# Two transformer blocks on one core: the grouped attentions' value product, row totals, score minima and weight remainders changed

## The chip, the cores and the metric

The kernel runs on one core of a Trainium2 chip. The metric is the device time of one execution in microseconds; lower is better. Below, PE is TensorE, DVE VectorE, ACT ScalarE, POOL GpSimd, and SP the engine that only issues transfers.

## The reference

Two blocks work on x of 512 tokens by 1024 channels, all in float32. The first has one layer: an RMS norm, a projection to queries, keys, values and gates, attention "a" (8 query heads on 2 key heads of 64, a window of 128 to either side, a slope times the distance subtracted from the scores, and one sink logit per head that takes part in the softmax), attention "b" (8 heads, a neighbourhood of 8 rows by 16 columns, with a table of relative biases, no sink), gated merging, an output projection, and an MLP with a squared relu of width 4096. The second has two layers. Each is a gated MLP of width 2816, a mixer, and another gated MLP. The mixer has a causal attention "c0" or "c1" (8 heads on 2, window 128, slopes and sinks as in a) beside a gated short convolution. A norm ends it.

```python
sc = q @ k * scale - slope * dist          # -inf outside the window
p  = exp(sc - m) / (sum(exp(sc - m)) + exp(sink - m))
out = p @ v                                # p has 128 queries x up to 384 keys per block and head
```

## The kernel before, in words

Everything lies transposed: x is 8 tiles of 128 channels by 512 tokens. Each weight tile (a "unit", 128 rows by 1024 columns, 512 KB) is fetched by SP into one of three places `w_raw`, and split in two: ACT writes the rounded part `w_hi` (line 890), and the rest `w_lo` is the difference (line 1084 on DVE, job `split_v`; line 1341 on POOL, job `split_g`, which is used while attentions run). Activations are split in the same way, and a dense product is three fp32r matmuls per 128 rows: hi·hi, lo·hi, hi·lo (lines 765 to 767), eight such steps per result.

The order of all work is written out once by the class `Plan`. A "slot" is the gap after one dense step of three matmuls; `later(n, job)` puts a small job n slots ahead, between dense steps. Each engine then runs its share of the same list of jobs in order, and waits on semaphores where a job needs another engine's result. `next_unit` adds the fetch of the unit three ahead at once and its split one slot later, so that a tile is split at the start of the next unit and used two units after its place came free. SP's list has the fetches (line 1417) in the same order as its other transfers.

One attention goes block by block (4 blocks of 128 queries), in two groups of four heads, a group every 10 slots (`attend`). For a group: four `score` jobs (PE, lines 779 on; two banks), each followed on DVE by the bias and the slope, read from PSUM into `probs` (line 1261, for b line 1256); `softmax` on DVE (reduction to the row maximum L1269, maximum with the sinks L1273, negation L1275, sink shift L1278); `exps` on ACT (L1018, with the row sums); then per chunk of 128 keys `turn` (PE transposes four 128x128 pieces of the probabilities, L793; ACT copies them out, L1031) and `multiply` (L806), three slots later, with the turned probabilities standing and 64 columns of values streaming, head by head, in plain fp32. `normalise` (DVE, L1286 to L1294) multiplies the bank of both groups by the inverse totals, `turn_out` transposes the result back (PE L817, ACT L1036) and `y_lo` takes its remainder. Attention a has 10 chunks per group of heads, b 8, c0 and c1 7 each.

All four attentions run among projections: a from about 50 to 165 us, b from about 170 to 265, c0 from about 1130 to 1215, c1 from about 2030 to 2115. The first block's bias table for b is loaded over POOL's queue (L1369) at 32 to 41 us.

## Time and profile before

| | us |
|---|---|
| median of 3 runs (2530.28 to 2532.93) | 2532.54 |
| the profiled execution's own time | 2533.4 |
| its span, first to last instruction | 2531.6 |
| PE, DVE, ACT, POOL busy | 2499.9, 1251.5, 895.7, 261.3 |
| mean TensorE clock granted | 0.996 |

A row of a group gives the line, engine and operation, the tiles out<-in with partitions x elements, the count after x, the busy time and the mean of one, and then the time the engine sat idle before them with what released it. A row of a timeline gives start, duration and the same names. Records of matmuls overlap, because they are pipelined, so their durations are longer than their distance. The window view gives busy times per stretch, the granted clock as a share of 2.4 GHz, and the DMA engines' share.

### The profile page before, as it was taken

To read this page: it belongs to the slowest core of one execution; us is meant where nothing else is said; L and a number is where in the kernel's file an instruction comes from. 1 tells how busy PE (TensorE), PEld (TensorE's weight loads), DVE (VectorE), ACT (ScalarE), POOL (GpSimd) and SP (SyncE) were. 2 spreads that over 40 slices of the span, in tenths; PEclk is the share of its full clock that TensorE was granted. 3 is DMA by queue.
4 is the path that set the end of the run, shared out by engine and by line. 5 is a ranking of instruction groups with operands and counts; after the bars stand their busy time and mean duration, and the time that the engine had idled before them with its cause. 6 is when DMAs were issued, how large, how long until landed. Compare 5 with 4: busy or idle time off the path is not lost.

```text
span 2531.6 us, 28151 instructions
## 1 busy us (share of the span) xinstructions
PE 2499.9 (99%) x11504; PEld 2073.0 (82%) x11504; DVE 1251.5 (49%) x1555; ACT 895.7 (35%) x1347; POOL 261.3 (10%) x179
## 2 busy tenths in 40 slices
PE   8999999999999999999999999999999999999998
PEld 7878888888888888878888888888888788888886
DVE  6664455434475343466454444543444665544444
ACT  5556343223343222344432222422222444322222
POOL 3243110000030000013300000100000143000001
PEclk9999999999999999999999999999999999999999
DMA  6112333233223333232233232333232322332322
GB/s 166 50 56 62 107 110 100 92 100 100 88 87 108 96 96 100 83 102 67 83 100 99 93 100 86 99 100 100 92 100 86 99 75 76 100 100 92 100 90 77
DMA packets 71167, 235.36 MB, mean 93 GB/s; under 512 B 8832, under 2 KB 12544, under 8 KB 71040
## 3 DMA queue, kind: packets, MB, share of 16 engines
q1 hardware_dynamic: 69376, 230.36, 29.4%
q0 software_dynamic: 1664, 3.22, 0.7%
q8 instruction: 91, 1.49, 0.2%
q14 instruction: 36, 0.29, 0.0%
HBM read 231.35 MB, written 2.19 MB: 92 GB/s over the span
## 4 chain that ended last, share of the span: by engine, by line
PE 88%; DVE 5%; ACT 3%; issue 3%; POOL 1%; DMA 0%; SPq 0%; DVEq 0%; ACTq 0%; POOLq 0%
PE bank L765 28%; PE bank L767 28%; PE bank L766 28%; PE bank L806 2%; DVE w_lo L1084 2%; ACT w_hi L890 1%; PE bank L779 1%; PE bank L793 1%; DVE x L1200 1%; DVE z L1076 1%; ACT z L878 0%; POOL square_sum L1351 0%; DVE q L1151 0%; DVE kb_lo L1164 0%; ACT h_hi L900 0%
## 5 line engine op out<-in xcount | busy, mean ns | idle before, releaser
L765 PE MATMUL bank<-h_hi,w_hi 128*128 128x512 f32 x2224 | 880.3, 396 | 3.8 <-DVE h_lo L1099 1.5
L767 PE MATMUL bank<-h_hi,w_lo 128*128 128x512 f32 x2224 | 868.0, 390 | 0.0
L766 PE MATMUL bank<-h_lo,w_hi 128*128 128x512 f32 x2224 | 867.4, 390 | 0.0
L1084 DVE TENSOR_TENSOR w_lo<-w_raw,w_hi 128x1024 fp32r<-128x1024 f32 (+2 forms) x392 | 485.4, 1239 | 319.4 <-ACT w_hi L890 318.8
L890 ACT ACTIVATE w_hi<-w_raw 128x1024 fp32r<-128x1024 f32 (+1 forms) x435 | 448.8, 1033 | 400.3 <-PE bank L767 397.9
L765 PEld LDWEIGHTS bank<-h_hi,w_hi 128*128 128x128 f32 x2224 | 418.9, 188 | 88.6 <-DVE w_lo L1084 4.5
L767 PEld LDWEIGHTS bank<-h_hi,w_lo 128*128 128x128 f32 x2224 | 418.1, 188 | 88.5
L766 PEld LDWEIGHTS bank<-h_lo,w_hi 128*128 128x128 f32 x2224 | 419.0, 188 | 81.2 <-issue 1.7
L767 PE MATMUL bank<-act_hi,w_lo 128*128 128x512 f32 x960 | 373.5, 389 | 0.0
L766 PE MATMUL bank<-act_lo,w_hi 128*128 128x512 f32 x960 | 373.5, 389 | 0.0
L765 PE MATMUL bank<-act_hi,w_hi 128*128 128x512 f32 x960 | 373.5, 389 | 0.0
L1076 DVE TENSOR_TENSOR z<-bank,rms_inv 128x512 f32<-128x512 f32 x238 | 168.6, 710 | 296.6 <-PE bank L767 295.8
L1351 POOL TENSOR_TENSOR square_sum<-square_sum,z 128x512 f32<-128x512 f32 x55 | 73.8, 1342 | 1839.4 <-ACT z L878 1839.4
L1200 DVE SCALAR_TENSOR_TENSOR x<-bank,x 128x512 f32<-128x512 f32 x152 | 104.7, 689 | 282.8 <-PE bank L767 282.8
L766 PEld LDWEIGHTS bank<-act_lo,w_hi 128*128 128x128 f32 x960 | 180.2, 188 | 37.5
L765 PEld LDWEIGHTS bank<-act_hi,w_hi 128*128 128x128 f32 x960 | 180.2, 188 | 37.5
L767 PEld LDWEIGHTS bank<-act_hi,w_lo 128*128 128x128 f32 x960 | 180.2, 188 | 37.2
L1007 ACT ACTIVATE act_hi<-z 128x512 fp32r<-128x512 f32 x88 | 55.6, 632 | 389.6 <-DVE z L1221 389.6
L1002 ACT ACTIVATE z<-z 128x512 f32<-128x512 f32 x88 | 55.6, 632 | 285.3 <-DVE z L1076 285.3
L1341 POOL TENSOR_TENSOR w_lo<-w_raw,w_hi 128x1024 fp32r<-128x1024 f32 x51 | 123.3, 2421 | 265.4 <-ACT w_hi L890 265.4
L1084 DVE TENSOR_TENSOR act_lo<-z,act_hi 128x512 fp32r<-128x512 f32 x120 | 83.2, 693 | 105.0 <-ACT act_hi L1007 61.4
L900 ACT ACTIVATE h_hi<-x,gains 128x512 fp32r<-128x512 f32 x56 | 40.6, 724 | 126.7 <-DVE x L1200 122.2
(169 smaller groups left out, 1678.0 us busy)
## 6 DMA issues: line engine op xcount, KB each, us to landing
w_raw<-ffn_wg_dram SPq DMA_DIRECT2D x88, 512.0 KB, 3.5
w_raw<-ffn_wu_dram SPq DMA_DIRECT2D x88, 512.0 KB, 3.5
w_raw<-w_in_dram SPq DMA_DIRECT2D x67, 512.0 KB, 3.6
w_raw<-ffn_wd_dram SPq DMA_DIRECT2D x64, 512.0 KB, 3.5
w_raw<-w_up_dram SPq DMA_DIRECT2D x32, 512.0 KB, 3.6
w_raw<-w_down_dram SPq DMA_DIRECT2D x32, 512.0 KB, 3.8
w_raw<-w_out_dram SPq DMA_DIRECT2D x24, 512.0 KB, 3.6
w_raw<-ffn_wd_dram SPq DMA_DIRECT2D x32, 384.0 KB, 3.2
```

What stands on the lines that cost most here:

```text
L765: engine.matmul(to, w_hi[s][:, lhs], hi, start=k == 0, stop=False)
L766: engine.matmul(to, w_hi[s][:, lhs], lo, start=False, stop=False)
L767: product = engine.matmul(to, w_lo[s][:, lhs], hi, start=False, stop=job == "k_last")
L806: product = engine.matmul(value_bank[:, half(place(name, h))], turned[0:rows, n * P:(n + 1) * P], values[name][0:rows, chunk, value_head(n ...
L890: engine.activation(w_hi[s][:, 0:width], w_raw[s][:, 0:width], ACT.Copy).then_inc(signals["w_hi"].s, 1)
L1002: engine.activation(z[zs[1] % Z_RING][:, :], z[zs[0] % Z_RING][:, :], ACT.Silu).then_inc(signals["silued"].s, 1)
L1007: engine.activation(act_hi[:, plan.hidden[key] % FF_RING, :], z[zs[1] % Z_RING][:, :], ACT.Copy).then_inc(signals["act_hi"].s, 1)
L1076: engine.tensor_tensor(to, src, scale, ALU.mult).then_inc(signals["evacuated"].s, 1)
L1084: engine.tensor_tensor(lo, value, hi.bitcast(F32), ALU.subtract).then_inc(signals[event].s, 1)
L1200: engine.scalar_tensor_tensor(x[:, m, :], dense_bank[plan.results[r].bank][:, :], factor(r), x[:, m, :], ALU.mult, ALU.add).then_inc(signa ...
L1341: engine.tensor_tensor(w_lo[s][:, 0:width], w_raw[s][:, 0:width], w_hi[s][:, 0:width].bitcast(F32), ALU.subtract).then_inc(signals["w_lo_g ...
L1351: engine.tensor_tensor(to, to, z[zs % Z_RING][:, :], ALU.add).then_inc(signals["scaled_sum" if scaled else "square_sum"].s, 1)
```

## The change

It has five parts. They concern a, c0 and c1 ("grouped") unless b is named.

1. Value product. The values of one key head now stand in the array as a 128x128 tile, 64 columns of the rounded part beside 64 of the remainder, and the turned probabilities of four heads stream over it, 512 columns, first their rounded part, then their remainder (new job `turn_lo` on DVE after ACT's copy; `v_lo` for the values). The bank holds the product transposed already: the lower 64 rows hold the remainder of the values. Job `pair` (ACT copies the lower half out, DVE adds it to the upper) ends each group, and `turn_out` is gone. b keeps its old form.
2. Totals. The inverse of the totals lies with queries on partitions, and the output now has channels there. SP stores the inverses to DRAM (`invert`), loads them back spread over the partitions (`inverse_in`, two transfers), and DVE multiplies (`weigh`).
3. Scores. The write of biased scores also keeps their lowest value, with the sign turned, and starts from the sink; reduction, maximum and negation are gone, and each exponential waits for its own head. This holds for b too. The distances come from DRAM multiplied by the slopes, per head: 1.5 MB for a (into tiles of x that are free), 1 MB each for c0 and c1, instead of 192 and 128 KB.
4. `split_g`. ACT writes the negated rounded part into `w_lo`, and a transfer on POOL's queue adds `w_raw` to it, instead of POOL's subtraction.
5. The scratch for POOL's descriptors is halved (4096 to 2048).

```diff
+GROUPED = ("a", "c0", "c1")
...
+        elif job == "exps" and key[0] in GROUPED and key[2] == 1:
+            self.later(1, "invert", *key[:2])
+            self.later(3, "inverse_in", *key[:2])
+        elif job == "turn" and key[0] in GROUPED:
+            self.later(1, "turn_lo", *key)
+        elif job == "v_turn" and key[1] is None:
+            self.later(1, "v_lo", *key)
+        elif job == "multiply" and key[0] in GROUPED and key[3] == len(CHUNKS[key[0]][key[1]]) - 1:
+            self.add("pair", key[:3])
+            if key[2] == 1:
+                self.later(2, "weigh", *key[:2])
+        elif job == "weigh":
+            self.later(1, "y_lo", *key)
+        elif job == "multiply" and key[0] == "b" and key[2:] == (1, len(CHUNKS[key[0]][key[1]]) - 1):
...
-            self.later(at + delay + 2 * len(chunks) + 5, "turn_out", name, i)
+            if name == "b":
+                self.later(at + delay + 2 * len(chunks) + 5, "turn_out", name, i)
...
+        self.add("far_1")
...
+                    va = sbuf("va", [P, BLOCKS, KV_HEADS, 2 * HEAD], F32R, part_a)
+                    turned_a_hi = sbuf("turned_a_hi", [P, 2, TOKENS], F32R, part_a)
+                    turned_a_lo = sbuf("turned_a_lo", [P, 2, TOKENS], F32R, part_a)
...
+            lower_2 = sbuf("lower_2", [HEAD, TOKENS], F32, on)
+            y_2 = sbuf("y_2", [P, TOKENS], F32, on)
+            inverse_2 = sbuf("inverse_2", [P, 2, TOKENS], F32, on)
...
+            far_2 = sbuf("far_2", [P, HEADS, 2 * BLOCK], F32, on)
+
+        far_1 = x[:, 0:6, :].rearrange("p a b -> p (a b)").rearrange("p (h n) -> p h n", h=HEADS)
...
+        lower_of = {"a": square_sum[0:HEAD, :], "c0": lower_2[:, :], "c1": lower_2[:, :]}
+        y_of = {"a": x[:, 6, :], "c0": y_2[:, :], "c1": y_2[:, :]}
...
+                return done("turn_lo" if key[0] in GROUPED else "turn_copied", key)
+            if job == "v_turn":
+                return done("v_lo" if key[1] is None else "v_copied", key)
+            return done("y_lo", key)
...
+                    if name in GROUPED:
+                        if c == 0:
+                            at = value_at["paired", key[:3]]
+                            pe.wait_ge(*done(*plan.values[at - 1]))
+                            pe.wait_ge(*done(*values_need(name)))
+                        at = chunk_at[key] % 2
+                        last = c == len(CHUNKS[name][i]) - 1
+                        pe.wait_ge(*done("turn_lo", key))
+                        engine.matmul(value_bank[:, :], values[name][:, chunk, g, :], turned_hi[name][:, at, :], start=c == 0, stop=False)
+                        engine.matmul(value_bank[:, :], values[name][:, chunk, g, :], turned_lo[name][:, at, :],
+                                      start=False, stop=last).then_inc(signals["multiplied"].s, 1)
+                        continue
...
+                    if job == "split_g":
+                        act.wait_ge(*done("w_hi", u))
+                        engine.activation(w_lo[s][:, 0:width], w_hi[s][:, 0:width].bitcast(F32), ACT.Copy, scale=-1.0).then_inc(signals["w_minus"].s, 1)
...
+                    if t is None:
+                        engine.activation(to[:, :, :, 0:HEAD], turn_bank[at % 2][:, :].rearrange("p (c h d) -> p c h d", c=BLOCKS, h=2),
+                                          ACT.Copy).then_inc(signals["v_copied"].s, 1)
+                        continue
...
+                        act.wait_ge(*done("biased", (*key, n)))
                         exps = engine.activation(probs[:, n, 0:count], probs[:, n, 0:count], ACT.Exp, bias=stats(neg_max, i, g)[:, n:n + 1],
-                                                 scale=EXP_SCALE[name], accum_out=row_sum[:, i % 2, at:at + 1])
+                                                 scale=-1.0, accum_out=row_sum[:, i % 2, at:at + 1])
...
+                elif job == "pair":
+                    name = key[0]
+                    act.wait_ge(*done("multiplied", (*key, len(CHUNKS[name][key[1]]) - 1)))
+                    if key in paired_before:
+                        act.wait_ge(*done("paired", paired_before[key]))
+                    engine.activation(lower_of[name], value_bank[HEAD:P, :], ACT.Copy).then_inc(signals["lower_copied"].s, 1)
+
+                elif job == "weigh":
+                    name, i = key
+                    act.wait_ge(*done("weighed", key))
+                    engine.activation(y_hi_of[name][:, :, block(i)], y_of[name].rearrange("p (t n) -> p t n", t=4), ACT.Copy).then_inc(signals["y_hi"].s, 1)
...
+                    engine.tensor_tensor_reduce(to, scores, away, -SCALE, most, ALU.add, ALU.min,
+                                                stats(neg_max, i, g)[:, n:n + 1]).then_inc(signals["biased"].s, 1)
...
+                elif job == "turn_lo":
+                    name, n = key[0], chunk_at[key] % 2
+                    v.wait_ge(*done("turn_copied", key))
+                    rest(turned_lo[name][:, n, :], turn_bank[turn_at["turn", key] % 2][:, :], turned_hi[name][:, n, :], "turn_lo")
+
+                elif job == "v_lo":
+                    to, at = values[name_of[key[0]]], turn_at["v_turn", key]
+                    v.wait_ge(*done("v_copied", key))
+                    rest(to[:, :, :, HEAD:2 * HEAD], turn_bank[at % 2][:, :].rearrange("p (c h d) -> p c h d", c=BLOCKS, h=2),
+                         to[:, :, :, 0:HEAD], "v_lo")
+
+                elif job == "pair":
+                    v.wait_ge(*done("lower_copied", key))
+                    engine.tensor_tensor(y_of[key[0]][half(key[2]), :], value_bank[0:HEAD, :], lower_of[key[0]], ALU.add).then_inc(signals["paired"].s, 1)
+
+                elif job == "invert":
+                    name, i = key
+                    total, inverse = row_sum[:, i % 2, :], row_inv[:, i % 2, :]
+                    v.wait_ge(*done("exped", (name, i, 1)))
+                    engine.tensor_tensor(total, total, sink_exp[:, i % 2, :], ALU.add).then_inc(signals["row_total"].s, 1)
+                    v.wait_ge(*done("row_total", key))
+                    if stats_before(name, i):
+                        v.wait_ge(*statistics_free(*stats_before(name, i)))
+                    engine.reciprocal(inverse, total).then_inc(signals["row_inv"].s, 1)
+
+                elif job == "weigh":
+                    name, i = key
+                    spread, landed_at, count = inverse_in(name, i)
+                    v.wait_ge(*done("paired", (name, i, 1)))
+                    v.wait_ge(landed_at, count)
+                    engine.tensor_tensor(y_of[name], y_of[name], spread, ALU.mult).then_inc(signals["weighed"].s, 1)
...
-                    pool.wait_ge(*done("w_hi", key))
-                    engine.tensor_tensor(w_lo[s][:, 0:width], w_raw[s][:, 0:width], w_hi[s][:, 0:width].bitcast(F32),
-                                         ALU.subtract).then_inc(signals["w_lo_g"].s, 1)
+                    pool.wait_ge(*done("w_minus", key))
+                    engine.dma_start(w_lo[s][:, 0:width].bitcast(F32), w_raw[s][:, 0:width], accum_op=ALU.add).then_inc(signals[f"w_added{s}"].s, 16)
...
+                elif job == "invert":
+                    name, i = key
+                    sp.wait_ge(*done("row_inv", key))
+                    engine.dma_start(dram["inverses"][inverse_at[key]].rearrange("h q -> q h"), row_inv[:, i % 2, :],
+                                     allow_slow_non_contiguous=True).then_inc(inverse_kept.s, 16)
+
+                elif job == "inverse_in":
+                    name, i = key
+                    n = inverse_at[key]
+                    spread, landed_at, _ = inverse_in(name, i)
+                    sp.wait_ge(inverse_kept.s, 16 * (n + 1))
+                    before = n - 1 if name == "a" else n - 2
+                    if before >= 0:
+                        sp.wait_ge(*done("weighed", plan.inverses[before]))
+                    for g in range(KV_HEADS):
+                        engine.dma_start(spread[half(g), :].rearrange("p (t n) -> p t n", t=GROUP),
+                                         dram["inverses"][n].rearrange("(t g) q -> g t q", g=KV_HEADS)[g].partition_broadcast(HEAD)).then_inc(landed_at, 16)
+
+                elif job == "far_1":
+                    sp.wait_ge(*done("h_lo", (0, KT - 1)))
+                    sp.wait_ge(*done("squared", (0, KT - 1)))
+                    engine.dma_start(far_1, dram["far_1"]).then_inc(in_landed["far_1"].s, 16)
...
+                    engine.dma_start(far_2[:, :, :], dram["far_2"]).then_inc(in_landed["far_2"].s, 16)
...
+    slopes = 2.0 ** -(np.arange(HEADS) + 1.0)[None, :, None] / SCALE
+    return ((-slopes * np.where(both <= BLOCK, both, MASKED)[:, None, :]).astype(np.float32),
+            (-slopes * np.where((past >= 0) & (past < BLOCK), past, MASKED)[:, None, :]).astype(np.float32))
```

## Rows read from the trace of the kernel before

**Rows 1.** The page, part 1: busy us, share of the span, instructions.
```profile
PE 2499.9 (99%) x11504; PEld 2073.0 (82%) x11504; DVE 1251.5 (49%) x1555; ACT 895.7 (35%) x1347; POOL 261.3 (10%) x179
```

**Rows 2.** The page, part 4: the chain that ended last, by engine.
```profile
PE 88%; DVE 5%; ACT 3%; issue 3%; POOL 1%; DMA 0%; SPq 0%; DVEq 0%; ACTq 0%; POOLq 0%
```

**Rows 3.** Groups by form, PE: records and time | busy us, mean ns | idle before.
```profile
L806 PE MATMUL bank<-v,probs_t 128*128 128x64 f32 x224 | 28.0, 268 | 0.0
...
L806 PE MATMUL bank<-va,probs_t 128*128 128x64 f32 x160 | 20.0, 268 | 0.0
...
L817 PE MATMUL bank<-identity,out_q 128*128 128x128 f32 x64 | 9.6, 272 | 0.0
```

**Rows 4.** Timeline of c0, all engines: start us, us, engine, line, what.
```profile
1151.95 0.39 PE L767 MATMUL bank<-h_hi,w_lo 128*128 128x512 f32 x1
...
1152.18 0.60 PE L817 MATMUL bank<-identity,out_q 128*128 128x128 f32 x4
...
1152.85 0.39 PE L766 MATMUL bank<-h_lo,w_hi 128*128 128x512 f32 x1
...
1158.37 0.39 PE L767 MATMUL bank<-h_hi,w_lo 128*128 128x512 f32 x1
...
1158.60 1.00 PE L806 MATMUL bank<-v,probs_t 128*128 128x64 f32 x8
...
1159.41 0.48 PE L765 MATMUL bank<-h_hi,w_hi 128*128 128x512 f32 x1
...
1159.72 0.39 PE L766 MATMUL bank<-h_lo,w_hi 128*128 128x512 f32 x1
```

**Rows 5.** Windows: PE, PEld, DVE, ACT, POOL busy (records), clock, DMA share, GB/s.
```profile
52.00:56.00 4.00, 1.22 (x4) 1.12 (x5) 3.07 (x6) 3.95 (x5) 1.98 (x1) 0.76 0.07 24
56.00:60.00 4.00, 4.00 (x11) 3.20 (x11) 2.50 (x7) 0.76 (x4) 2.85 (x2) 0.50 0.47 140
...
132.00:136.00 4.00, 0.73 (x4) 0.26 (x2) 3.94 (x5) 0.57 (x2) 2.86 (x1) 1.00 0.00 0
```

**Rows 6.** Groups by form, DVE: busy us, mean ns | idle before.
```profile
L1269 DVE TENSOR_REDUCE row_max<-probs 128x4 f32<-128x1024 f32 x20 | 24.4, 1220 | 0.7
...
L1273 DVE TENSOR_TENSOR row_max<-row_max,sinks 128x4 f32<-128x4 f32 x24 | 13.9, 578 | 0.8
...
L1084 DVE TENSOR_TENSOR q<-bank,q 128x512 fp32r<-128x512 f32 x8 | 5.5, 688 | 3.2 <-ACT q L1036 3.2
```

**Rows 7.** Groups by form, ACT: busy us, mean ns | idle before.
```profile
L890 ACT ACTIVATE w_hi<-w_raw 128x1024 fp32r<-128x1024 f32 x403 | 422.5, 1049 | 381.7 <-PE bank L767 379.3 <-DMA w_raw<-w_in_dram 2.0
...
L1031 ACT ACTIVATE probs_t<-bank 128x512 f32<-128x512 f32 x60 | 35.6, 595 | 73.3 <-PE bank L793 73.2
...
L1018 ACT ACTIVATION_READ_ACCUMULATOR probs<-probs,neg_max 128x1 f32 x128 | 23.9, 187 | 0.0
```

**Rows 8.** Timeline of DVE in a: the remainders of kb, four together.
```profile
110.52 2.78 DVE L1164 TENSOR_TENSOR kb_lo<-z,kb_hi 64x512 fp32r<-64x512 f32 x4
...
130.74 4.83 DVE L1164 TENSOR_TENSOR kb_lo<-z,kb_hi 64x512 fp32r<-64x512 f32 x4 [3.88 <-ACT kb_hi L957]
```

**Rows 9.** Timeline of POOL in b: the subtraction of weights (a third lies between).
```profile
204.22 2.40 POOL L1341 TENSOR_TENSOR w_lo<-w_raw,w_hi 128x1024 fp32r<-128x1024 f32 x1 [10.09 <-ACT w_hi L890]
...
217.50 2.37 POOL L1341 TENSOR_TENSOR w_lo<-w_raw,w_hi 128x1024 fp32r<-128x1024 f32 x1 [5.31 <-ACT w_hi L890]
```

**Rows 10.** DMA issues: count, KB each, median us to landing; last: 33 to 48 us.
```profile
x<-x_dram POOLq DMA_DIRECT2D x8, 256.0 KB, 3.1
...
rel_scratch_dram<-z SPq DMA_DIRECT2D x1, 94.0 KB, 2.1
...
w_raw<-w_in_dram SPq DMA_DIRECT2D x1, 512.0 KB, 10.4
```

**Rows 11.** Timeline of c0: last exponential and last product of block 0.
```profile
1142.62 0.19 ACT L1022 ACTIVATE sink_exp<-sink_shift 128x4 f32<-128x4 f32 x1
...
1148.52 1.00 PE L806 MATMUL bank<-v,probs_t 128*128 128x64 f32 x8
```

More of the change, by code:

```diff
@@ L141, in __init__ @@
         self.turns, self.values, self.scores, self.groups, self.chunks = [], [], [], {}, {}
-        self.slot, self.beside = 0, []
+        self.slot, self.beside, self.inverses = 0, [], []
         self.current, self.ready_results, self.pending_norm = 0, [], None
@@ L182, in run @@
             self.turns.append((job, key))
-        if job == "multiply" and key[2:] == (0, 0):
+        if job == "multiply" and key[0] in GROUPED and key[3] == 0:
+            self.values.append(("paired", key[:3]))
+        if job == "multiply" and key[0] == "b" and key[2:] == (0, 0):
             self.values.append(("normalised", key[:2]))
+        if job == "invert":
+            self.inverses.append(key)
         if job == "score":
@@ L536, in two_blocks @@
         ones = sbuf("ones", [P, P])
-        dist_1 = sbuf("dist_1", [P, 3 * BLOCK])
         eps_col = sbuf("eps_col", [P, 1])
@@ L620, in two_blocks @@
         in_landed = {name: signal(f"{name}_landed", 16) for name in
-                     ("gains", "identity", "dist_1", "sinks", "gate_bias", "conv_w", "dist_2", "rel", "bias")}
+                     ("gains", "identity", "far_1", "sinks", "gate_bias", "conv_w", "far_2", "rel", "bias")}
         signals["rel_kept"] = signal("rel_kept", 16)
+        for i in range(UNITS_HELD):
+            signals[f"w_added{i}"] = signal(f"w_added{i}", 16)
         out_stored = signal("out_stored", 16)
+        inverse_kept = signal("inverse_kept", 16)
+        inverse_landed = [signal(f"inverse_landed{n}", 16) for n in range(2)]
         units = plan_units(dram)
@@ L677, in two_blocks, with inverse_in, statistics_free @@
         chunk_at = {key: n for of in plan.chunks.values() for n, key in enumerate(of)}
+        inverse_at = {key: n for n, key in enumerate(plan.inverses)}
+        paired_before = {}
+        for name in GROUPED:
+            of = [key for job, key in plan.values if job == "paired" and BUFFERS[key[0]] == BUFFERS[name]]
+            paired_before.update(zip(of[1:], of))
+        def inverse_in(name, i):
+            n = inverse_at[name, i]
+            spread = x[:, 7, :] if name == "a" else inverse_2[:, n % 2, :]
+            return spread, inverse_landed[n % 2].s, 32 * (n // 2 + 1)
+        def statistics_free(name, i):
+            if name in GROUPED:
+                return inverse_kept.s, 16 * (inverse_at[name, i] + 1)
+            return done("normalised", (name, i))
         def turn_freed(n):
@@ L1255, in vector_program @@
                         v.wait_ge(*done("bias_masked", (1 if i == 2 else i, g)))
-                        biased = engine.scalar_tensor_tensor(to, scores, SCALE, masked_bias[:, h, 0:count], ALU.mult, ALU.add)
+                        away, most = masked_bias[:, h, 0:count], MASKED
                     else:
-                        dist, dist_in = (dist_1, in_landed["dist_1"]) if name == "a" else (dist_2, in_landed["dist_2"])
+                        far, far_in = (far_1, in_landed["far_1"]) if name == "a" else (far_2, in_landed["far_2"])
@@ L1259, in vector_program @@
                         first = BLOCK if i == 0 else 0
-                        v.wait_ge(dist_in.s, 32 if name == "c1" else 16)
-                        biased = engine.scalar_tensor_tensor(to, dist[:, first:first + count], -(2.0 ** -(h + 1)) / SCALE, scores, ALU.mult, ALU.add)
-                    biased.then_inc(signals["biased"].s, 1)
+                        v.wait_ge(far_in.s, 32 if name == "c1" else 16)
+                        v.wait_ge(*done("neg_sinks", ()))
+                        away, most = far[:, h, first:first + count], neg_sinks[:, SINK[name], h:h + 1]
@@ L1295, in vector_program @@
                                          ALU.mult).then_inc(signals["normalised"].s, 1)
+                elif job == "y_lo" and key[0] in GROUPED:
+                    name, i = key
+                    v.wait_ge(*done("y_hi", key))
+                    rest(y_lo_of[name][:, :, block(i)], y_of[name].rearrange("p (t n) -> p t n", t=4), y_hi_of[name][:, :, block(i)], "y_lo")
                 elif job == "y_lo":
@@ L1550 @@
     gains.append(a["final_norm_2"])
-    dist_1, dist_2 = distances()
+    far_1, far_2 = distances()
     arrays = {
```

115 lines of the change are left out of this document (51 added, 64 removed).

## The prediction

> **What bounds the kernel now.** I read the page's busy shares first, then the chain of work that ended last, then TensorE's groups by form, and only then the timeline of one attention. PE is busy 99% of the span, the chain is PE for 88% of it, and DVE (49%) and ACT (35%) have room on average [rows 1, 2]. So the time moves if PE gets less to do, or if an in-order DVE, ACT, POOL or SP makes PE wait where it does not wait now. The records don't give PE's price: a dense matmul is recorded with nearly 400 ns, but its successor starts 0.23 us after it (1158.37 to 1158.60) [rows 4]. I price PE work by starts.
>
> PE idles only 2531.6 - 2499.9 = 31.7 us. The windows show the two dearest places, both in the first attention: PE busy 1.22 of 4 us at 52 to 56, with the clock granted at 0.50 (1.2 GHz) in the next window, and 0.73 of 4 us at 132 to 136 [rows 5]. In both, scores wait for DVE's biased writes. In the attentions of the second block PE has no such hole.
>
> **The change part by part, PE.** *Value products.* The grouped attentions now issue 8 records per chunk (4 heads, each in two records), 224/8 = 28 chunks in c0 and c1 and 160/8 = 20 in a, 48 in all [rows 3]. One chunk costs: from L767 at 1158.37 to L766 at 1159.72 are 1.35 us, with two dense steps of 0.23 in it, so 0.89 us [rows 4]. The new chunk is two matmuls of the dense form (standing 128x128, 512 columns, fp32r): 2 x 0.23 = 0.46. Gain 0.43 x 48 = 20.6 us.
>
> *Turning the output back.* Four transposes per block: 1151.95 to 1152.85 is 0.90, less two dense steps 0.44 us [rows 4]. 64/4 = 16 blocks have them [rows 3], only b's 4 keep them: 12 x 0.44 = 5.3 us. Scores and the turning of probabilities stay. PE's sum: 25.9 us less, on a path that is PE.
>
> The Trainium skill, "TensorE: Matmul & The Clock Gate", section "Back-to-back issue gap", gives about 131 ns per matmul of 512 columns in a sustained stream. By it the new chunks would cost 0.26 us and 9 us more would be gained; the trace has 0.23 us for the same form, so the sum goes by the trace.
>
> **DVE.** Gone: the reductions over a group's scores (20 of 1220 ns in the commonest form), the maximum with the sinks (24 of 578 ns), 32 scalings of these few values and 12 normalisations [rows 6]. I take 32 x 1.2 + 24 x 0.58 + 32 x 0.25 + 12 x 0.69 = 69 us. Added: 48 remainders of turned probabilities, 24 pair additions, 12 weighings, 3 value remainders, each a 512-wide operation like the 688 ns one [rows 6]: 87 x 0.69 = 60 us; and 128 score writes that also keep their lowest value. No row shows that instruction; from below it costs nothing more than the write it replaces, from above as much again as the removed reduction per head, 1.22/4 = 0.3 us; I take 0.19, ACT's read of its accumulator [rows 7], so 24 us. Net +15 us. Against that POOL no longer reads SBUF for the weights: kb_lo's four operations took 4.83 us beside POOL and 2.78 without [rows 8], about 2 us back each time. DVE comes out about even in load. What matters more: a group's exponentials no longer wait for 1.2 us of reduction and the maximum behind the last score, so they start that much earlier.
>
> **ACT.** 51 tiles get a second pass of 1.05 us [rows 7], 54 us, and 24 copies of a half bank at 0.6, 14 us. Cover: ACT's idle time while PE streams. Queued behind a pass are turned copies and exponentials. A turned chunk is multiplied 3 slots (9 dense steps, 2.1 us) and its interleaved work after it is turned; copy 0.60 [rows 7] plus remainder 0.69 fit with 0.8 us to spare and more where scores lie between. Without this cover each chunk would wait the rest of a pass.
>
> **Weights by transfer.** Now POOL subtracts in 2.4 us [rows 9]. New: negated copy 1.05, then a transfer on POOL's queue that adds w_raw to it. An adding transfer has no row. Bound from below: POOL's 256 KB load, 3.1 us; from above: a 512 KB load in the crowded stretch, 10.4 us [rows 10]. I take 5, nearest the quiet load. A tile is split one slot after its place is free and used two units later. The closest two spacings in b are 204.22 to 217.50, 13.3 us [rows 9]; less a slot (0.7) that leaves 12.6 for 1.05 + 1.05 + transfer. So it is hidden up to a landing of 10.5 us, and costs nothing at 5. The next fetch into w_raw waits for it as well, but has a further unit. POOL itself gets shorter, so the masks of b come sooner (up to 1 us of gain, kept for the range).
>
> **Totals by transfer.** On SP, per block, one store of inverses in single values and two broadcast loads; fetches stand behind both waits, with a unit (8 us) in hand. Store from below 2.1 us (the store to the scratch), loads each like it; from above 10.4 each [rows 10]. I take 2.5 + 3.5 with two issues. From block 0's last exponential at 1142.81 to its last product at 1148.52 [rows 11], and the product's 1 us and two slots, there are about 8 us (1148.52 + 1.0 + 1.4 - 1142.81); later blocks have one chunk (two slots and more) extra, about 11. 6 to 7 us fit: zero, with 1 to 2 us of margin. Without it DVE stands in the weighing, and evacuations and scores queue behind.
>
> **Loads of the distances.** far_1 is 1.5 MB on SP behind unit 6, before the stretch with the 10.4 us load; far_2 1 MB twice. Fetches have about two units in hand; nothing later than scores needs them. From 0 to 3 us; I take 1, at the first stall, with the value remainder (0.69) ahead of the scores there.
>
> **Sum.** 2533.4 (the profiled execution's own time; span 2531.6, median of the runs 2532.5) - 25.9 + 1 for the first stall + 2 for a new short wait in c0 and c1 (late copies and pairs) = 2510.5. Against the median a little less: **2510 us**.
>
> **The rivals.** *Crowding (0.20).* Every chunk has a DVE hop more and every bank of values an ACT and a DVE hop, in order with everything else. For: 68 us more of ACT in stretches where it now waits little; PE runs ahead faster. Against: no hole in c0 and c1 now. If 48 chunks lose 0.25 us each, 12 us are given back: 2522; a new idle spell as at 52 to 56, with its slow clock, adds some 5.
>
> *The holes close (0.13).* Earlier exponentials and 2 us less in front of the scores at 132 to 136 take away that stall and other short ones (waits for the turned output's bank vanish with it): up to 7 us more, 2503.
>
> *A chunk costs little more than one dense step (0.02).* Its two matmuls use the same standing values, so the second could follow faster than dense ones, whose weights change each time. At 0.26 per chunk 48 x 0.2 = 9.6 us more are gained, 2501. Against: the dense stream beside them holds 0.23, and 64-wide and 128-wide products with fresh weights start closer than that, so the load is not what sets it. The Trainium skill's page "TensorE: Matmul & The Clock Gate" has the faster pace.
>
> *The adding transfer is the bound (0.07, slower).* It decides from a landing of 10.5 us in the closest units, about 13 where units take 8 us. At 14 us each of 51 tiles makes PE wait 1 to 3.5 us, about 100 in all plus slow clock, less the 26: 2600. For: reading source and target, from POOL, may be far slower than a load. Against: the DMA engines carry 0.07 and 0.00 of their time in two of the three windows shown [rows 5].
>
> *The round trip is late (0.06, same or slower).* From 8 us in block 0 of c0 and c1 and about 11 in the ten others DVE stands still at the weighing, and PE soon after, for want of biased scores. At 12 us that is 2 x 4 + 10 x 1 = 18 us, 2528; at 13 us 2 x 5 + 10 x 2 = 30 us, 2540.
>
> **The numbers.** Forecast case 0.52, 2505 to 2516. Range 2502 to 2526: it leaves out the slow rivals (0.13), the tail of crowding, and little below. A measurement of this kernel tells about 0.2% (5 us) from nothing. Faster: 0.52 + 0.13 + 0.02 + crowding but its tail (0.17) = 0.84; same 0.06; slower 0.10.
>
> **What would show it.** Right: two value matmuls per chunk, starts 0.23 us apart, no transposes of out_q in a, c0, c1; c0's stretch shorter by about 7 us with PE free of holes; added transfers landing under 8 us with nobody waiting; DVE's weighing not waiting on DMA. Wrong: PE idle with w_lo's transfer or the weighing as releaser; PE's waits for turned remainders or pairs summing over 10 us; a second or third window at half clock.

## The result and the profile after

The changed kernel takes 2682.4 us, the median of 4 runs (2679.8 to 2682.9), against 2532.7 for the kernel before; the ratio is 1.059 [1.058, 1.061]. It was to be 2510, and at most 2526. It is 150 us slower.

The page of the changed kernel: busy time, then slices of the span, then the chain that ended last.

```profile
PE 2503.9 (93%) x11168; PEld 2062.0 (77%) x11168; DVE 1234.5 (46%) x1670; ACT 962.9 (36%) x1422; POOL 182.6 (7%) x179
...
PE   8669999999999999976799999999999966999998
...
PEclk9889999999999999998899999999999987999999
...
PE 78%; DMA 6%; DVE 5%; ACT 5%; issue 4%; POOL 1%; SPq 0%; DVEq 0%; ACTq 0%; POOLq 0%
```

PE was busy 99% [rows 1] and is busy 93%; its idle time rose from 32 to 177 us. The losses lie in three places of the slices, which are the three grouped attentions. DMA, absent from the chain before [rows 2], holds 6% of it.

To compare stages I take the start of the same dense matmul in both traces. The first row of each pair is the kernel before, the second the changed one; the columns are those of [rows 5]. First attention a, then c0, then c1:

```profile
58.36:201.96 143.60, 135.00 (x766) 114.49 (x764) 86.48 (x136) 81.14 (x178) 47.09 (x23) 0.98 0.18 58
1117.12:1255.81 138.69, 138.09 (x730) 116.95 (x729) 78.31 (x132) 62.63 (x135) 48.00 (x26) 1.00 0.24 77
2010.75:2135.91 125.16, 124.56 (x669) 105.68 (x668) 69.75 (x124) 58.38 (x129) 43.98 (x23) 1.00 0.24 75
```
```profile
57.77:242.19 184.42, 134.73 (x630) 108.54 (x628) 76.81 (x173) 102.12 (x204) 23.57 (x22) 0.86 0.41 95
1157.37:1352.50 195.13, 142.31 (x629) 115.77 (x628) 77.74 (x162) 81.06 (x157) 28.52 (x26) 0.85 0.42 95
2107.49:2285.54 178.05, 124.80 (x570) 101.53 (x568) 69.53 (x155) 76.44 (x150) 24.49 (x23) 0.86 0.43 97
```

The three stages grew by 41, 56 and 53 us, which is the whole 150. Outside them nothing moved by more than 1 us. PE issues 99 to 136 records fewer in each, as foreseen, but its busy time doesn't fall, because the clock granted over the stages drops to 0.85 and 0.86 of full speed: behind the long idle spells PE runs for a while at 1.2 GHz, as the rows below show. DVE and POOL have less to do than before, ACT 18 to 21 us more per stage.

Where a stage is lost shows in c0. First SP's line over this stretch of the plan in the kernel before, then SP, ACT and PE in the changed kernel:

```profile
1112.43 60.33 SPq L1417 DMA_DIRECT2D w_raw<-w_in_dram  x10
```
```profile
1152.65 12.50 SPq L1529 DMA_DIRECT2D w_raw<-w_in_dram  x3
1184.21 0.38 SPq L1550 DMA_DIRECT2D inverses_dram<-row_inv  x1
1184.63 0.58 SPq L1529 DMA_DIRECT2D w_raw<-w_in_dram  x1
1195.77 1.25 SPq L1562 DMA_DIRECT2D inverse<-inverses_dram  x2
1197.06 1.08 SPq L1529 DMA_DIRECT2D w_raw<-w_in_dram  x2
```
```profile
1197.27 1.06 ACT L956 ACTIVATE w_hi<-w_raw 128x1024 fp32r<-128x1024 f32 x1 [13.52 <-DMA w_raw<-w_in_dram]
```
```profile
1200.90 0.77 PE L861 MATMUL bank<-turned_hi,v 128*128 128x512 f32 x1 [11.78 <-DVE turned_lo L1174]
1201.47 0.63 PE L862 MATMUL bank<-turned_lo,v 128*128 128x512 f32 x1
1201.89 0.63 PE L819 MATMUL bank<-h_hi,w_hi 128*128 128x512 f32 x1
```

In the kernel before, ten fetches of SP went out over 60 us with none of its other transfers between them. In the changed kernel SP has issued its last fetch by 1165.15 (1152.65 + 12.50) and then stands until 1184.21 for the inverses. The next fetch follows the store at once, at 1184.63, but lands only 12.6 us later, at about 1197.27, where ACT has idled 13.5 us for it. ACT works in order, so exponentials and copies of turned chunks stand behind that split; PE idles 11.8 us for turned_lo and then runs dense matmuls 0.43 us apart instead of 0.23 (the clock granted from 1196 to 1200 us is 0.50 of full speed, 1.2 GHz). The page's transfers and the waits of SP and ACT show both parts of the round trip (us in total, times, longest):

```profile
w_lo<-w_raw POOLq DMA_DIRECT2D x51, 512.0 KB, 4.4
...
inverse<-inverses_dram SPq DMA_DIRECT2D x16, 128.0 KB, 3.1
...
inverses_dram<-row_inv SPq DMA_DIRECT2D x12, 4.0 KB, 11.2
```
```profile
SPq L1550 <- DVE row_inv L1386: 244.0, 12, 23.7
...
SPq L1562 <- DMA inverses_dram<-row_inv: 127.6, 12, 12.5
```
```profile
ACT w_hi L956 <- DMA w_raw<-w_in_dram: 112.4, 11, 15.2
```

The store of 4 KB takes 11.2 us, three times a 512 KB fetch. It goes out as single values: packets under 512 bytes are 22512, against 9649 without the round trip, 12863 more, of which 12 x 1024 are the stores'. Four of the twelve stores had a fetch right behind them, and these four fetches landed after 12.5 to 13.9 us, where the median of this transfer is 4.0. Behind the other eight stores, all four of a among them, the two loads come next in SP's list, so that no fetch could be issued for the 10 to 13 us of the store. The weighing on DVE, which the prediction watched, never waited for its loads.

The sum of 244.0 us is no measure of the loss by itself. SP also stood 398.5 us in the kernel before, for POOL's w_lo, and 155.2 us remain of that now (for the adding transfer): SP stands about as long as before, but in other places. Which of its stands cost time has to come from the experiments.

### The profile page after: what moved, and what is told of

It is laid out like the page before. It is cut to its first block, busy times and chain, and to the rows that moved or that the text cites. A ratio compares the mean times of both kernels' runs of the same rounds, so it can differ in the third digit from the quotient of the medians.

```text
span 2680.8 us, 27714 instructions
## 1 busy us (share of the span) xinstructions
PE 2503.9 (93%) x11168; PEld 2062.0 (77%) x11168; DVE 1234.5 (46%) x1670; ACT 962.9 (36%) x1422; POOL 182.6 (7%) x179
## 2 busy tenths in 40 slices
DMA packets 97519, 268.50 MB, mean 100 GB/s; under 512 B 22512, under 2 KB 31984, under 8 KB 97008
## 4 chain that ended last, share of the span: by engine, by line
PE 78%; DMA 6%; DVE 5%; ACT 5%; issue 4%; POOL 1%; SPq 0%; DVEq 0%; ACTq 0%; POOLq 0%
PE bank L819 25%; PE bank L820 25%; PE bank L821 25%; DMA inverses_dram<-row_inv 3%; DMA w_raw<-w_in_dram 3%; ACT w_hi L956 2%; DVE w_lo L1174 1%; ACT probs L1091 1%; PE bank L833 1%; DVE x L1290 1%; PE bank L847 1%; PE bank L872 1%; DVE z L1166 0%; ACT z L944 0%; POOL square_sum L1462 0%
## 5 line engine op out<-in xcount | busy, mean ns | idle before, releaser
L1453 POOL DMA_DIRECT2D w_lo<-w_raw x51 | 44.3, 868 | 467.9 <-ACT w_lo L959 467.9
```

The costliest lines, as they stand in the source:

```text
L1453: engine.dma_start(w_lo[s][:, 0:width].bitcast(F32), w_raw[s][:, 0:width], accum_op=ALU.add).then_inc(signals[f"w_added{s}"].s, 16)
```

## The experiments

Each ran beside the kernel before (2532 to 2533 us in each group). "Stage ends" are the shifts in us of the ends of a, c0 and c1 against the kernel before by the same dense matmuls, each less the shift at the end of the stage before it; the changed kernel has +40.2, +56.5, +52.9. They come from one traced execution of each kernel. The figure of a counts from the program's start, and the time up to the start of a alone differed by up to 1.8 us between traces.

**No round trip.** The store, the loads and their waits are gone; the weighing multiplies by another tile of the same shape, so the kernel leaves out the division by the totals.

```diff
-  (SP: store of row_inv, wait, two loads)
-                    v.wait_ge(landed_at, count)
-  ... y_of[name], spread, ALU.mult
+  ... y_of[name], rms_inv[:, :], ALU.mult
```

> Leaves out the transfers of the totals: the output of a, c0 and c1 is multiplied by another tile in memory, so it is not normalised; everything else is as changed. Theory Q (SP's queue: the store of single values lands after 11 us, the fetch issued behind it lands 12.6 us later, and fetches wait behind SP's two waits, so ACT stands before late weight tiles and everything behind it in order is late): the 150 us go and the sum of the prediction shows, 2510 +- 6. Rival C (crowding: the extra hops over ACT and DVE are the loss): at least 2560. Rival W (the adding transfer holds up the weights): at least 2560, with PE waiting for w_lo.

Measured 2535.0 (10 runs), ratio 1.001 [1.000, 1.002]; stage ends +13.7, -5.2, -5.1. So the round trip costs 147 us and nothing else in the change is near that. But the gain of 25 does not appear either (2510 was expected here): c0 and c1 are 5 us shorter, and a is 14 longer. Waits of PE in this kernel, and a stretch of a (ACT, DVE, PE):

```profile
PE bank L833 <- DVE neg_max L1353: 23.7, 9, 7.5
PE bank L861 <- DVE turned_a_lo L1174: 6.1, 6, 1.7
```
```profile
85.07 0.62 ACT L1091 ACTIVATE probs<-probs,neg_max 128x384 f32<-128x384 f32 x1
...
87.57 1.04 ACT L956 ACTIVATE w_hi<-w_raw 128x1024 fp32r<-128x1024 f32 x1
88.65 1.06 ACT L959 ACTIVATE w_lo<-w_hi 128x1024 fp32r<-128x1024 f32 x1
89.73 0.59 ACT L1114 ACTIVATE square_sum<-bank 64x512 f32<-64x512 f32 x1
```
```profile
90.36 0.68 DVE L1376 TENSOR_TENSOR x<-bank,square_sum 64x512 f32<-64x512 f32 x1 [8.20 <-ACT square_sum L1114]
91.07 2.79 DVE L1254 TENSOR_TENSOR kb_lo<-z,kb_hi 64x512 fp32r<-64x512 f32 x4
93.89 0.69 DVE L1392 TENSOR_TENSOR x<-x,rms_inv 128x512 f32<-128x512 f32 x1
```
```profile
96.56 0.69 PE L833 MATMUL bank<-ka_hi,qa 128*128 128x384 f32 x1 [7.14 <-DVE neg_max L1353]
```

ACT reaches the copy of the lower half (L1114) only after four exponentials and two passes of a weight tile. DVE stands 8.2 us at the addition of the halves (L1376), with kb's remainders and the next block's scores behind it, and PE idles 7.1 us at the score.

**The store in rows of 32 bytes.** The totals go out as they lie, 8 values per query, and are read back in a shape that costs the same (a load lands after 3.3 us, 3.1 in the changed kernel). The kernel leaves out putting heads and queries back in their order.

```diff
-  dma_start(dram["inverses"][n].rearrange("h q -> q h"), row_inv[:, i % 2, :], ...)
+  dma_start(dram["inverses_q"][n], row_inv[:, i % 2, :])
```

> The store of the inverses writes each query's 8 values in one piece (128 pieces of 32 bytes, not 1024 of 4), with the loads as before; so heads and queries are mixed up in the totals' order, the work is the same otherwise. Q with the store's length as the cause: the store lands in 2 to 3 us, the time falls to within 10 us of the kernel without the transfers. Q with SP's standing at the row_inv wait as the cause (fetches behind a wait for ACT and DVE's results): the store is short, but the time stays over 2560.

2589.4 (one run); the store lands in 1.4 us; stage ends +17.0, +18.0, +21.2.

**The totals turned first.** DVE turns row_inv in 32 x 32 squares, and four stores of 8 x 128 bytes follow.

```diff
+  engine.transpose(turned_inv[:, i % 2, :], row_inv[:, i % 2, :])   # DVE
+  for b in range(4):
+      dma_start(dram["inverses"][n][:, 32*b:32*b+32], turned_inv[32*b:32*b+HEADS, i % 2, :])
```

> DVE turns the inverses in 32x32 blocks before the store, which then goes in four transfers of 8 rows of 128 bytes; the output is the reference's. Q with the store's length as the cause: stores land in about 2 us, 2510 to 2520, faster than both kernels. Q with the row_inv wait as the cause: over 2560. Rivals C and W: over 2560 as well.

2599.4 (4 runs), ratio 1.026 [1.025, 1.028]; stage ends +18.1, +25.7, +22.6. Waits of SP and ACT:

```profile
SPq L1556 <- DVE turned_inv L1391: 262.6, 12, 31.9
...
SPq L1567 <- DMA inverses_dram<-turned_inv: 10.3, 12, 1.3
```
```profile
ACT w_hi L957 <- DMA w_raw<-w_in_dram: 47.6, 10, 7.9
```

With a quick store 83 (this) or 93 us (rows of 32 bytes, one run) of the 147 are gone: that is what the slow store costs. SP still stands 263 us for the inverses, ACT still waits for fetches, and 54 to 64 us remain over the kernel without the round trip.

**The loads late.** As the change, but the two loads 9 slots later in SP's list, the weighing 3 later, and one more wait on DVE before the next block's addition.

```diff
-            self.later(3, "inverse_in", *key[:2])
+            self.later(12, "inverse_in", *key[:2])
-                self.later(2, "weigh", *key[:2])
+                self.later(5, "weigh", *key[:2])
```

> Store as changed, but its loads stand 9 slots later in SP's list (and the weighing 3 slots later, with a wait before the next block's pair). SP no longer stands 11 us for the store before it can issue the next fetch; the fetch issued just behind the store still shares its rings. If the wait for the store is the cause, 2520 to 2560; if the rings filled with single values and the row_inv wait are, 2620 or more.

2649.2 (one run); stage ends +26.1, +46.5, +43.5. This is 33 us less than the changed kernel, and above the 2520 to 2560 expected if the wait for the store were the cause. The wait for the store falls only from 127.6 to 122.0: in most blocks the fetches between store and loads are overdue by SP's stand and go out within about 1 us, so SP is at the wait again while the store is still under way. And a fetch issued early gains little: all twelve that followed a store by 0.4 us landed after 12.4 to 13.6 us. Which of the moved parts gives the 33 us back is not shown.

**Another queue.** The turned totals with the four stores and two loads on GpSimd's queue, 1 and 4 slots behind the inverse.

```diff
-  (SP: "invert", "inverse_in")
+            self.later(2, "inverse_out", *key[:2])   # POOL: wait, 4 stores
+            self.later(5, "inverse_in", *key[:2])    # POOL: wait, 2 loads
```

> The turned totals (2599.35) with their four stores and two fetches issued from GpSimd's queue, 1 and 4 slots behind the inverse, instead of SyncE's; all is computed. Theory S (what the round trip still costs after the store is made short is SyncE standing at the inverse with the fetches of weights behind it, 64 us): the time falls to that of the kernel without the round trip plus a little, 2535 to 2545, with no wait of ScalarE for w_raw. Rival D (it is the transfers themselves or VectorE's waiting for them): 2580 to 2600, with VectorE waiting at the weighing; or GpSimd now stands before the adding transfers, and w_lo is late: TensorE waits on w_lo and 2560 to 2600.

2543.9 (4 runs), ratio 1.005 [1.003, 1.006]; stage ends +13.7, -0.5, -1.3. SP's line and the transfers:

```profile
1126.14 67.16 SPq L1553 DMA_DIRECT2D w_raw<-w_in_dram  x10
```
```profile
inverse<-inverses_dram POOLq DMA_DIRECT2D x16, 128.0 KB, 4.2
x<-inverses_dram POOLq DMA_DIRECT2D x8, 128.0 KB, 3.8
inverses_dram<-turned_inv POOLq DMA_DIRECT2D x48, 1.0 KB, 2.6
```

The same arithmetic and bytes as the run with the turned totals (2599.4), 55.5 us less; the stores and loads also stand 1 and 2 slots later. Ten fetches stand in one row again, and of ACT's waits for w_raw 2.2 us are left, as in the kernel before (2.0). So SP's stand is the other cause. The round trip still costs 9 us (against none), and DVE's four waits for the loads of c0 and c1 at the weighing, which the run with the turned totals did not have, sum to 8.7 us, the longest 3.9.

**The addition later, no round trip.** ACT's copy of the lower half stays, DVE's addition comes 4 slots behind it.

```diff
+            self.later(4, "pair_add", *key[:3])      # DVE's half of "pair"
-                self.later(2, "weigh", *key[:2])
+                self.later(6, "weigh", *key[:2])
```

> The kernel without the round trip (2535.0), with VectorE's adding of the two halves placed 4 slots behind ScalarE's copy of the lower half, and the weighing 6 slots behind instead of 2. Theory L (VectorE stands in its line at the adding for a ScalarE that is 8 us behind, with the scores of the next block, for which TensorE waits, queued behind it; the waits on neg_max of 23.7 us in 9 times and the half clock after them are that): the waits on neg_max fall below 8 us and the time to 2505 to 2520. Rival A (ScalarE is short of time in attention a whatever the order, as its second pass of 1.06 us per unit is added there): the waits move from neg_max to sink_exp and turned_a_hi, and the time stays within 2530 to 2536.

2528.7 (10 runs), ratio 0.9986 [0.9976, 0.9996]; stage ends -0.1, -3.3, -1.8. In a, 14 us come back, 1.8 of them ahead of the stage; so DVE's stand at the addition was that loss of attention a (the weighing moved with it, which no run separates). In c0 and c1 the same move costs 2 to 3 us. The waits on neg_max halve (12.2 us, 7 times), not fall below 8, and the time stays above the 2520 expected: the mechanism holds, its share was put too high.

**GpSimd's subtraction back, no round trip.**

```diff
-  ACT: w_lo = -w_hi ; POOL queue: w_lo += w_raw
+  POOL: w_lo = w_raw - w_hi
```

> The kernel without the round trip (2535.0), with w_lo taken again by GpSimd's subtraction: ScalarE loses 51 passes of 1.06 us (54 us), the queue its 51 adding transfers; GpSimd gets 51 subtractions back. Rival A (ScalarE short of time): 2505 to 2520. Theory L (the order is at fault, the crowding only makes it longer): a few us at most, 2527 to 2536, with neg_max waits left at over 12 us. If the adding transfers by their DMA traffic held something up, waits of SyncE for w_lo would fall from 410 us, at no change of the time.

2546.2 (4 runs), ratio 1.006 [1.004, 1.007]; stage ends +18.4, -3.3, -1.8. Both theories are wrong here: it is 11 us slower than with the transfer, though ACT loses 54 us of work. Two groups of DVE, first with the subtraction, then (the run without round trip) with the transfer:

```profile
L1247 DVE TENSOR_TENSOR kb_lo<-z,kb_hi 64x512 fp32r<-64x512 f32 x16 | 15.0, 936 | 0.4 <-ACT kb_hi L1023 0.2
L1247 DVE TENSOR_TENSOR qb<-z,qb 64x512 fp32r<-64x512 f32 x8 | 9.7, 1212 | 0.9 <-ACT qb L1023 0.7
```
```profile
L1254 DVE TENSOR_TENSOR kb_lo<-z,kb_hi 64x512 fp32r<-64x512 f32 x16 | 11.0, 685 | 0.3
L1254 DVE TENSOR_TENSOR qb<-z,qb 64x512 fp32r<-64x512 f32 x8 | 5.5, 686 | 0.9 <-ACT qb L1030 0.7
```

DVE's operations with both inputs in SBUF take 1.4 to 1.8 times as long in the mean; those that read a bank (turned_a_lo, 688 and 687 ns) don't change. It is the ones that meet POOL's subtraction: of four rows of kb_lo in a, the one beside which POOL is idle takes 2.78 us, the other three 3.7 to 4.8. By the stage ends 5 of the 11 us fall in a, where that work stands between PE and its scores, and 5 in c0 and c1: there cv_lo goes from 690 to 1237 ns and PE's waits for it from 0.6 to 3.6 us.

**The transfer alone, on the kernel before.** The same edit the other way round, nothing else.

> The kernel before (2532) with one part of the change alone: in attention w_lo is ScalarE's negated copy of w_hi with w_raw added by a transfer, instead of GpSimd's subtraction. On the kernel without the round trip this part was worth 11.3 us (2546.2 with GpSimd's subtraction, 2535.0 with the transfer), and VectorE's subtractions between SBUF tiles took 685 instead of 936 to 1212 ns. If that is a gain of its own: 2522 to 2530. If ScalarE's second pass costs attention a what VectorE gains (before keeps ScalarE short of nothing): 2530 to 2536. If ScalarE becomes late: above 2537.

2530.3 (10 runs), ratio 0.9992 [0.9983, 1.0001]: no difference that can be told, so the second case expected. In the trace a ends 3.6 us earlier, 1.4 of it gained before a starts; c0 and c1 stay where they were. What the transfer was worth in the kernel without the round trip (11 us) it is not worth here; the reason is open.

**Both repairs.** The kernel of the other queue with the later addition.

> Both repairs at once, all is computed: the turned totals by GpSimd's queue and the adding 4 slots, the weighing 6 slots later. If theories L and S both hold: 2508 to 2525, which is faster than the kernel before (2532) and after (2682). If S alone holds: 2532 to 2545. If neither: 2580 or more.

2532.0 (10 runs), ratio 1.000 [0.999, 1.001]; stage ends +1.2, -2.9, -1.6. Against the changed kernel that is 150 us less, yet no gain over the kernel before is left to see: S holds, L in part. The transfers cost 2 us against the run without them and with the same addition, by the stage ends.

**The inverse later, and kb's remainders later.** Two more moves of the same kind on top; the stores and loads move with the inverse.

```diff
-            self.later(1, "invert", *key[:2])
+            self.later(5, "invert", *key[:2])
-        self.later(2, "project_lo", what, t)       (second run only)
+        self.later(4, "project_lo", what, t)
```

> The kernel of both repairs (2532.0) with VectorE's inverse 5 slots behind ScalarE's last exponential instead of 1, the store and the fetches moved by the same 4 slots. Theory L goes on (what is left of the loss in attention a is VectorE standing in its line for ScalarE at other places; at the inverse it stands 2.56 and 1.38 us in 110 to 160 us): 2524 to 2530, and the waits of row_sum for sink_exp gone. Rival (VectorE only stands elsewhere then, or the weighing becomes late): 2530 to 2540.

> As the run of the later inverse, and VectorE's four subtractions for kb and qb 4 slots behind their tile instead of 2 (at 131.87 us it stood 2.62 us for ScalarE's kb_hi, then took 2.79 us, with four scores behind, and TensorE's longest wait of 4.0 us for neg_max is that). Theory L: 3 to 6 us less than the run of the later inverse, 2520 to 2527. Rival: the subtractions of 2.8 us in one piece, not the standing, are what the scores wait for: no change within 2 us.

2543.2 (5 runs) and 2545.2 (4 runs), ratios 1.005 [1.003, 1.006] and 1.005 [1.004, 1.007]: worse, against theory L. Stage ends -1.6, +4.2, +4.2 and +3.7, +4.6, +4.4. In c0 and c1 the later inverse costs 6 to 7 us, where PE's two waits for DVE's q grow from 5.2 to 8.1 us and those for turned_lo from 1.4 to 4.1. DVE's waits in the first of the two runs name what ended them:

```profile
DVE y L1400 <- DMA inverse<-inverses_dram: 11.6, 4, 3.5
```

In the run of both repairs this was 0.7 us. With the inverse later, the loads land too late for the weighing: this is the rival expected ("the weighing becomes late"), and the prediction's rival of a late round trip, in c0 and c1 alone. In a the later inverse ends the stage 2.8 us earlier, and moving kb's remainders takes 5 us back, each by a single trace; the executions of the first run spread over 9 us (2539.7 to 2549.0), and the two medians differ by 2.0, so these two shares are uncertain. A move has to be judged for each stage.

**Each move where it helped.** Addition and inverse later in a only; in c0 and c1 where the change has them; the weighing 6 slots behind the products everywhere.

```diff
+            wait = 4 if key[0] == "a" else 0
+            self.later(wait + 1, "invert", *key[:2])
...
+            self.later(4 if key[0] == "a" else 0, "pair_add", *key[:3])
```

> The two repairs, each set where the traces showed it to help, all is computed: in attention a the adding 4 slots and the inverse 5 slots later (against the kernel before, that stage ended 1.6 us earlier in the run of the later inverse, 1.2 later without it, 13.7 later with neither), in c0 and c1 both in the places of the change (they ended 0.5 and 0.8 us earlier there with the weighing 2 slots behind, which once waited 3.9 us for a fetch, and 5.2 and 5.1 us earlier without a round trip), with the weighing 6 slots behind. Theory L, order stage by stage: -1.6 and twice -2.5 to -4.5, so 2522 to 2526. Rival (each move only shifts the standing to another place of the line, as the later inverse did in c0): 2530 or more.

2525.1 (7 runs, 2523.7 to 2528.8), ratio 0.9974 [0.9963, 0.9985]: 7 us faster than the kernel before in its group (2532.1), 157 us faster than the changed one; stage ends -0.9, -4.1, -4.3. Its windows over the same matmuls, PE's waits, and two of PE's waits in the kernel before:

```profile
58.36:201.04 142.68, 127.21 (x629) 101.79 (x628) 79.03 (x177) 101.91 (x205) 37.62 (x46) 0.98 0.53 124
1116.22:1250.81 134.59, 130.87 (x629) 107.84 (x628) 78.69 (x166) 80.90 (x157) 42.25 (x50) 1.00 0.55 137
2005.75:2126.61 120.86, 117.11 (x570) 96.64 (x568) 70.38 (x159) 76.23 (x150) 38.17 (x47) 1.00 0.59 142
```
```profile
PE bank L837 <- DVE neg_max L1358: 10.4, 6, 3.5
PE bank L865 <- DVE turned_a_lo L1179: 6.7, 7, 1.9
PE bank L823 <- DVE q L1179: 3.5, 2, 1.8
PE bank L851 <- DVE turned_a_lo L1179: 2.9, 1, 2.9
...
PE bank L865 <- DVE turned_lo L1179: 1.4, 4, 0.4
```
```profile
PE bank L779 <- DVE probs L1261: 8.0, 4, 3.4
...
PE bank L793 <- ACT probs_t L1031: 1.5, 1, 1.5
```

PE's busy time is 7.8, 7.2 and 7.5 us below that of before over the same matmuls, 22.5 together. Its idle time in the stages is 15.5, 3.7 and 3.8 against 8.6, 0.6 and 0.6, so 13.1 more. The difference is the 9.3 us by which the stages are shorter in these two traces. Most of the new idle time is for turned remainders: 6.7 + 2.9 + 1.4 = 11.0 us, where PE waited 1.5 for the turned copies before; in front of scores it waits 10.4 us against 9.2 (8.0 and 1.2 for b). In c0 and c1 the one difference from the run with the other queue is the weighing 4 slots later: these stages end 3.6 and 3.0 us earlier for it, and DVE's waits for the loads there fall from 8.7 to 0.6 us.

## Why the prediction was wrong

**PE's sum, 25.9 us less: right, a little high.** Two value matmuls per chunk stand 0.23 us apart at full clock, and in the best version 22.5 us of PE's busy time are gone. Of c0's 14 chunks and 4 turnings 7.8 were expected and 7.2 measured; of a's 20 chunks and 4 turnings 10.4 and 7.8, with half-clock stretches in both. The rival of a cheaper chunk is out: of the 48 pairs in the changed kernel none stands closer than 0.226 us.

**"Totals by transfer", put at "zero, with 1 to 2 us of margin", is the step that failed.** Two things in it were wrong.

First the size. The store was taken at 2.5 us, near the bound of 2.1 from a store of 94 KB in long rows. Its form has no row in the trace of before, and it measured 11.2 us, beyond even the upper bound of 10.4. It also delays what is behind it: the fetch issued 0.4 us later took 12.6 us instead of about 4. Shortening it alone gives back 83 to 93 us. The size alone would not have led to the measured time: with 11.2 + 3.1 us in the prediction's own rule for a late round trip, 2 x 6.3 + 10 x 3.3 = 46 us are lost, an estimate of 2556.

Then the place. "Fetches stand behind both waits, with a unit (8 us) in hand" was said and not worked through. SP runs ahead of ACT and DVE in its list; it reaches the wait for the inverses up to 23.7 us before they exist (31.9 in the run with turned totals), and the fetches behind it lose that lead. A margin of 8 us doesn't cover it. Even with a quick store this costs 55 us, shown by the pair of runs that differ in the queue and 1 to 2 slots (2599.4 to 2543.9). The prediction looked at who consumes the totals, DVE at the weighing, and priced that rival by a landing of 12 or 13 us, at 2528 to 2540; in the changed kernel DVE never waited there. The price lay with those queued behind the waiting instruction: SP, then ACT, then PE and its clock.

**The adding transfer: right.** 5 us were taken, 4.4 measured, and no wait of TensorE names it. The rival on the slower side that hung on it is out; SP's waits for w_lo are as long with the transfer as with the subtraction (410.8 and 409.4 us without the round trip).

**ACT's and DVE's extra work, 3 us: too low, about 13.** The rival of crowding had it (12 us given back, 2522), and with its mechanism: the repaired kernel stands at 2525, and PE's waits for turned remainders sum to 11.0 us, over the 10 that the prediction named as a sign of being wrong. That is the state after the moves. In the changed order there is one loss more that the text did not price: it counted the addition of the halves as load, and 2 us for late pairs in c0 and c1, but nothing for where the addition stands in a. There DVE waits for an ACT that has exponentials and two passes of a weight tile in front: 8.2 us in one case, 14 us of the time together with the slow clock. In c0 and c1 nothing of the kind is lost.

**POOL's port: right in sign; its worth depends on the kernel.** "About 2 us back each time" was said of kb_lo and entered no sum. The four rows of kb_lo lose 4 us together (15.1 to 11.0). The time gains 11 us in the kernel without round trip, but under 2, within the noise, in the kernel before. DVE's load was to rise by 15 us before this; its busy time fell from 1251.5 to 1234.5.

**The distances: no cost seen, 1 us taken.** The first score of a starts at 47.8 us in the changed kernel and at 49.0 before, and the first stall behind it is 3.5 us against 3.4.

**The holes close: not seen.** PE idles 15 us in attention a in the best version, against 8.6 before. The stall at 52 to 56 us stays (3.5 against 3.4), the one at 132 to 136 is 7.5 in the changed kernel and 2.2 in the best version, against 3.3. The score writes (part 3) were not taken back alone, so what they are worth is open, as is the smaller scratch (part 5).

## What to carry to other kernels

When a wait is put into the list of an in-order queue, work out where that queue stands at that moment, not when the consumer needs the data: a queue that fetches ahead gives up its whole lead at the first wait for a fresh result. Put such a transfer on a queue that runs in step with its producer, and early enough for its consumer. Count a transfer by its pieces, and turn a small tile on chip before it is stored; and when an operation is split over two engines, leave slots between the halves, each stage judged on its own.

## What the runs showed of the hardware

A store of 4 KB from 128 partitions as 1024 single values lands in 11.2 us, the same 4 KB in 128 pieces of 32 bytes in 1.4 us. A 512 KB fetch issued 0.4 us behind the first on the same queue landed after 12.5 to 13.9 us, four times of four, against a median of 4.0. What the DMA engines do in that time the traces don't settle: the packets of 4 bytes are recorded in the first 2 us, and from 1188 to 1192 us, where the engines' share is 0.51 at only 37 GB/s, all 36 packets recorded are larger than 2 KB and so belong to the fetch. Over c0 in the kernel before, the share is 0.24 at 77 GB/s.

A transfer that adds 512 KB from one SBUF tile to another lands in 4.4 us and leaves DVE alone, whereas GpSimd's subtraction of the same tile raises the means of DVE's groups with both inputs in SBUF from 685 to 936 ns (kb_lo) and from 686 to 1212 ns (qb); with an input in PSUM they stay (687 and 688).

DVE's write that also keeps the lowest value took 480 ns for 256 columns and 616 for 384, where the write without it took 420 and 553; with 83 ns for the read of the kept value that is about 0.14 us more, less than the 0.19 us taken from ACT's read.
